# Two narrow weight sums moved behind the low halves of a group's plain slots

## The reference

```python
def hybrid_layer(x, ...):
    h = rms_norm(x, norm_mix)
    proj = h @ w_in                              # 2048 x 5656
    ...
    x = x + mix @ w_out                          # 2048 x 2048
    hf = rms_norm(x, norm_ffn)
    gate, up = jnp.split(hf @ w_gu, 2, axis=-1)  # 2048 x 11264
    return x + (jax.nn.silu(gate) * up) @ w_down # 5632 x 2048
```

## Time and profile before

| what | value |
|---|---|
| time, median of 3 executions | 1097.41 us (1097.21 to 1098.8) |
| the profiled execution | 1097.72 us, span 1096.0 us |
| TensorE busy | 1084.9 us, 5071 matmuls |
| VectorE busy | 888.4 us, 1092 instructions |
| ScalarE busy | 598.8 us, 736 instructions |
| TensorE's granted clock | 0.999 of full speed |
| `raw` loads of `w_gu` | 176, 512 KB each, median 4.2 us from issue to landing |
| `raw` loads of `w_down` | 88, 512 KB each, median 4.6 us |

### The profile page before, as it was taken

One profiled execution on the slowest core, in us unless ns is written; L12 is line 12 of the kernel. 1 busy time (PEld: TensorE's weight loads), 2 busy tenths in 40 slices (PEclk: granted clock), 3 DMA queues, 4 the chain that ended last, 5 costly groups with the idle time before them and its releaser, 6 DMA issues.

```text
span 1096.0 us, 13959 instructions
## 1 busy us (share of the span) xinstructions
PE 1084.9 (99%) x5071; PEld 902.9 (82%) x5071; DVE 888.4 (81%) x1092; ACT 598.8 (55%) x736; POOL 40.7 (4%) x68
## 2 busy tenths in 40 slices
PE   9999999999999999999999999999999999999997
PEld 7897889888888888888888888888888878888885
DVE  5556866688756557999999999999998999899896
ACT  5655545555545445555655555556556555646553
POOL 2600000000010000000000000000000000000000
PEclk9999999999999999999999999999999999999999
DMA  8665646565546675656566566556666856666663
GB/s 290 214 199 168 186 131 179 161 173 154 181 163 235 188 253 171 204 185 210 189 199 214 165 208 206 185 184 209 210 192 197 301 190 215 203 200 209 200 224 117
DMA packets 110948, 215.39 MB, mean 197 GB/s; under 512 B 6957, under 2 KB 11633, under 8 KB 110001
## 3 DMA queue, kind: packets, MB, share of 16 engines
q1 hardware_dynamic: 108976, 205.36, 59.1%
q0 software_dynamic: 1632, 8.96, 2.2%
q10 hardware_dynamic: 288, 0.39, 0.1%
HBM read 210.49 MB, written 4.19 MB: 196 GB/s over the span
## 4 chain that ended last, share of the span: by engine, by line
PE 92%; DVE 4%; DMA 2%; issue 1%; ACT 1%; SPq 0%; POOLq 0%; POOL 0%; DVEq 0%; ACTq 0%
PE acc L1454 11%; PE acc L1455 11%; PE acc L1456 11%; PE acc L1735 10%; PE acc L1734 10%; PE acc L1736 10%; PE acc L1805 4%; PE acc L1807 4%; PE acc L1806 4%; PE mx L1734 3%; PE mx L1735 2%; PE mx L1736 2%; PE mx L1446 2%; PE mx L1805 1%; PE mx L1807 1%; PE mx L1806 1%
## 5 line engine op out<-in xcount | busy, mean ns | idle before, releaser
L786 DVE TENSOR_TENSOR w_lo<-raw,w_hi 128x1024 fp32r<-128x1024 f32 (+2 forms) x144 | 166.4, 1169 | 120.2 <-ACT w_hi L473 119.5
L473 ACT ACTIVATE w_hi<-raw 128x1024 fp32r<-128x1024 f32 (+2 forms) x143 | 143.2, 1013 | 135.4 <-PE acc L1456 129.0
L1734 PE MATMUL acc<-w_hi,hT_hi 128*128 128x512 f32 x460 | 179.9, 391 | 0.0
L1735 PE MATMUL acc<-w_lo,hT_hi 128*128 128x512 f32 x460 | 179.1, 389 | 0.0
L1736 PE MATMUL acc<-w_hi,hT_lo 128*128 128x512 f32 x460 | 179.0, 389 | 0.0
L1221 DVE TENSOR_TENSOR w_lo<-raw,w_hi 128x1024 fp32r<-128x1024 f32 (+1 forms) x160 | 173.3, 1119 | 2.8
L673 ACT ACTIVATE w_hi<-raw 128x1024 fp32r<-128x1024 f32 (+1 forms) x160 | 151.5, 978 | 36.7 <-PE acc L1736 21.8
L1454 PE MATMUL acc<-w_hi,hT_hi 128*128 128x512 f32 (+2 forms) x416 | 157.7, 379 | 0.0
L1456 PE MATMUL acc<-w_hi,hT_lo 128*128 128x512 f32 (+2 forms) x416 | 155.5, 374 | 0.0
L1455 PE MATMUL acc<-w_lo,hT_hi 128*128 128x512 f32 (+2 forms) x416 | 155.5, 374 | 0.0
L679 ACT ACTIVATE w_hi<-ff_sum 128x1024 fp32r<-128x1024 f32 x60 | 63.8, 1063 | 78.3 <-PE acc L1736 65.2
(11 more groups left out here) (317 smaller groups left out, 1682.5 us busy)
## 6 DMA issues: line engine op xcount, KB each, us to landing
raw<-in_w_gu SPq DMA_DIRECT2D x176, 512.0 KB, 4.2
raw<-in_w_down SPq DMA_DIRECT2D x88, 512.0 KB, 4.6
raw<-in_w_in SPq DMA_DIRECT2D x79, 512.0 KB, 4.0
raw<-in_w_out SPq DMA_DIRECT2D x32, 512.0 KB, 4.3
raw<-in_w_in SPq DMA_DIRECT2D x8, 272.0 KB, 2.8
raw<-in_w_in SPq DMA_DIRECT2D x8, 264.0 KB, 2.8
x<-in_x POOLq DMA_DIRECT2D x2, 1024.0 KB, 9.5
x_kept<-x POOLq DMA_DIRECT2D x2, 1024.0 KB, 7.3
```

The costliest lines, as they stand in the source:

```text
L786: dve.tensor_tensor(w_lo[:, slot, 0:UC * width], raw[:, slot, 0:UC * width], w_hi[:, slot, 0:UC * width].bitcast(F32), ALU.subtract).then_ ...
L1734: pe.matmul(o, a[0], w[0], start=first, stop=False)
L1735: pe.matmul(o, a[0], w[1], start=False, stop=False)
```

## The change

VectorE's order within a group changes. `ff_weight_sums` and `weight_sums` keep the wide sum alone. The two narrow sums become functions of their own, `ff_last_sums` and `last_sums`, which are called behind the low halves of the group's two plain slots and ahead of the low half of the wide sum. In the FFN's first group the activation sums (`act_sums`, `act_low`) keep their place ahead of the plain slots' low halves, so they now follow the wide sum directly. As the narrow sums read the raw slots after the low halves do, SyncE waits for the last sum as well before it loads into a raw slot of a group. The two tables `FF_SUMS_OF` and `SUMS_OF` say which loads that are, and the count to wait for.

```diff
--- before.py
+++ after.py
@@ -69,6 +69,7 @@
     FF_SLOT_OF[_i] = _v
     if _kind == "seven":
         FF_SLOT_OF[_i + 1] = _v + 1
+FF_SUMS_OF = {_i + d: 2 * _k + 2 for _kind, _k, _i, _v in FF_ORDER if _kind == "seven" for d in range(2)}
 
 
 def lin(j, m, c=0):
@@ -137,6 +138,8 @@
     SLOT_OF[_q] = _v
     if _kind in ("pair", "seven"):
         SLOT_OF[_q + 1] = _v + 1
+SUMMED_AT = [_q for _kind, _half, _k, _q, _v in DOWN if _kind == "seven"]
+SUMS_OF = {_q + d: 2 * n + 2 for n, _q in enumerate(SUMMED_AT) for d in range(2)}
 LAST_SEVEN = [max(i for i, d in enumerate(DOWN) if d[0] == "seven" and d[1] == h) for h in range(2)]
 FIRST_RIGHT = [i for i, d in enumerate(DOWN) if d[1] == 1][0]
 SPLIT = [(0, 5), (5, 7), (7, SUMMED)]
@@ -321,6 +324,9 @@
                 load(w_gu, U_FF + k, k % R, (k % UPG) * UC * P, FF if k >= UPG else 0, GW)
 
             def load_ff(j, k, i, up):
+                summed = FF_SUMS_OF.get(i - R)
+                if summed is not None:
+                    sp.wait_ge(sem("ff_w_sums"), (j - 1) * 2 * FF_SUMMED + summed)
                 sp.wait_ge(lo_ready, j * FF_SLOTS + (FF_BASE + FF_SLOT_OF[i - R] + 1))
                 sp.dma_start(raw[:, i % R, :].rearrange("p (k n) -> p k n", k=UC),
                              weights(w_gu, k * UC * P, j * GW + (FF if up else 0), GW)).then_inc(loaded[i % R], 16)
@@ -334,6 +340,8 @@
                         load_ff(j, k, i, kind == "up")
 
             def load_down(n, k, q):
+                if q - R in SUMS_OF:
+                    sp.wait_ge(sem("w_sums"), SUMS_OF[q - R])
                 sp.wait_ge(lo_ready, SLOT_OF.get(q - R, V_DN + q - R - U_DN) + 1)
                 sp.dma_start(raw[:, q % R, :].rearrange("p (k n) -> p k n", k=UC),
                              weights(w_down, k * UC * P, n * GW, GW)).then_inc(loaded[q % R], 16)
@@ -1242,6 +1250,10 @@
                 upper = raw[:, a:a + 2, 0:GW] if b > a else raw[:, a::b - a, 0:GW]
                 dve.tensor_tensor(ff_sum[:, 0, :, :], raw[:, b, :].rearrange("p (k n) -> p k n", k=UC), upper,
                                   ALU.subtract).then_inc(sem("ff_w_sums"), 1)
+
+            def ff_last_sums(j, i, k):
+
+                a, b = i % R, (i + 1) % R
                 dve.wait_ge(sem("ff_w_sums"), lin(j, 2 * FF_SUMMED, 2 * (k - FF_SUMMED) + 1))
                 dve.tensor_tensor(ff_sum[:, 1, 0, :], raw[:, b, GW:2 * GW], ff_sum[:, 0, 0, :], ALU.subtract)\
                    .then_inc(sem("ff_t2"), 1)
@@ -1281,6 +1293,7 @@
                     ff_low(j, i, v)
                     if kind == "seven":
                         ff_low(j, i + 1, v + 1, GW)
+                        ff_last_sums(j, i, k)
                         ff_sum_low(j, 0, v + 2)
                         ff_sum_low(j, 1, v + 3)
                     if kind == "gate" and k == 4:
@@ -1338,6 +1351,10 @@
                 dve.wait_ge(loaded[a + 1], 16 * (q // R + 1))
                 dve.tensor_tensor(gate_s[:, :, :], raw[:, a + 1, :].rearrange("p (k n) -> p k n", k=UC),
                                   raw[:, a:a + 2, 0:GW], ALU.subtract).then_inc(sem("w_sums"), 1)
+
+            def last_sums(q, made):
+
+                a = q % R
                 dve.wait_ge(sem("actT_psum"), NG_FF)
                 dve.wait_ge(sem("w_sums"), made - 1)
                 step(dve.tensor_tensor(act_tok[:, 0, :], raw[:, a + 1, GW:2 * GW], gate_s[:, 0, :], ALU.subtract))
@@ -1397,6 +1414,7 @@
                         for b in range(NB):
                             down_add(0, b, v - 2)
                     down_low(v + 1, q + 1, GW)
+                    last_sums(q, 2 * sevens)
                     sum_low(v + 2, gate_s)
                     if i == FIRST_RIGHT:
                         for b in range(NB):
```

## The result

| kernel | median | runs | range |
|---|---|---|---|
| before | 1097.31 us | 6 | 1096.54 to 1098.8 us |
| changed | 1101.93 us | 6 | 1101.28 to 1102.83 us |

The ratio is 1.0041, 95% interval 1.003 to 1.0051. The change costs 4.6 us where the forecast's case said +1.3. The time lies inside the predicted range (1093.8 to 1103.5), but beyond the 2.2 us that were called "same", and outside the forecast case's own range (1096.5 to 1100.5). It is the outcome "slower", which had 0.32. The profiled execution took 1101.67 us, with a span of 1099.9 us and a granted clock of 0.998.

What follows compares the result with a forecast made beforehand. TensorE, busy 1084.9 of 1096.0 us, was taken to bound the kernel, so only its waits could change. Third groups -3.5, first groups +4.8 and down stage 0 made +1.3 us on 1097.4: 1098.7 us, range 1093.8 to 1103.5.

Steps and rivals of the forecast that it cites:

- the forecast's case: Whole kernel: +1.3 us, to 1098.7 us, with its own range 1096.5 to 1100.5; chance 0.60.
- slower: Whole kernel: outcome of a slowdown beyond the 2.2 us a measurement can tell from no change; chance 0.32.
- Loads set the pace: FFN loop and down stage: loads released later hold up the next group's sums; likely 1101 to 1104 us, chance 0.27.
- Third groups: Third group of each FFN pass: first slot ready 1.45 us earlier, ending ten waits of 0.35 us; -3.5 us.
- First groups: First group of nine FFN passes: narrow sums lose their cover, third slot is late, 0.53 us each; +4.8 us.
- Now VectorE idles until 692.00: FFN first group: VectorE waits behind the wide sum for ScalarE's copies, ending at 691.97, before the activation sums start.
- Order within a group: VectorE, from the wide sum's start: third slot ready after 5.43 us instead of 5.55, first after 2.36 instead of 3.81.
- Later release in the FFN loop: FFN loop: second group's loads wait for narrow sums; third group's third slot keeps a 0.2 us margin, costed at nothing.
- Down stage: Down stage: second group's wait moves from first slot to third; bounds -1.0 and +1.5 us, taken as 0.
- The wait just goes: First group's third slot is in time after all, if ready 0.36 us earlier; 1093 to 1094 us, chance 0.13.
- The ring: Down stage: issue, landing and sums total 9.6 us at median landing, against TensorE's 10.2; binds when landings exceed 5.2 us.
- The profile I had asked for: Signs of right: third-group waits gone, nine new first-group waits about 0.4 us, VectorE idle, down-stage wait at wide sum's low half.

Runs made afterwards that it cites:

- e11: Kernel before with the new order in the third group of each FFN pass only; 1094.62 us, ratio 0.9975.
- e4: Changed kernel with the FFN's hardware loop over the middle eight passes written out; 1098.66 us, ratio 1.001.
- e5: Kernel before with the FFN's hardware loop written out; 1098.05 us, ratio 1.0004.
- e6: e3 with ScalarE's copy for the down stage moved one up slot earlier; 1094.58 us, ratio 0.9966.
- e1: Changed kernel with the change kept in the FFN loop only, the down stage as before; 1102.46 us, ratio 1.004.
- e12: Kernel before, order unchanged, with only a group's first raw slot released 0.6 us later, together with its second; 1098.82 us, ratio 1.0015.
- e10: Kernel before, order unchanged, with both raw slots of a group reloaded only once the third slot's low half is made; 1145.19 us, ratio 1.0428.
- e2: Changed kernel with the change kept in the down stage only, the FFN loop as before; 1097.55 us, ratio 0.9999.
- e7: Kernel before with the change in third groups of the FFN loop and in the down stage; 1095.07 us, ratio 0.9978.
- e3: Changed kernel, but in each pass's first group both narrow sums and the raw slot releases stand as before; 1094.63 us, ratio 0.9972.
- e8: Changed kernel, but in first groups narrow sum 1 alone goes ahead of the activation sums, narrow sum 2 staying behind the low halves; 1094.97 us, ratio 0.9977.
- e9: e3 with the FFN's hardware loop written out; 1093.53 us, ratio 0.9966.

## Why the prediction was right in its mechanism and short in its size

- **The number.** 1101.93 is inside the stated range in part by luck. The forecast's case ended at 1100.5; the range went further for the rival "Loads set the pace" (1101 to 1104), whose mechanism is not what made the time.
- **Third groups.** Right. All ten waits are gone, -3.3 us against -3.5. e11 has this part alone and is 3.0 us faster than before.
- **First groups.** The mechanism, place and count are right: nine passes pay, the last does not, no second wait follows. The size is off: 0.75 to 0.81 us in eight of them against 0.53. The step that failed is "Now VectorE idles until 692.00". I took the start behind ScalarE's copy as 0.03 after its end. Measured are 0.25 in the loop and 0.10 with constants (e4). Together with a low half that reached TensorE after 0.13 instead of 0.06 in every other pass, this is about the 1.8 us between 4.8 and 6.6. e4 with e5 shows that the loop's form of the code makes it: -3.3 us for writing out the changed kernel, +0.3 (nothing) for the kernel before. The 0.03 was right for an instruction that carries its wait itself (L1227); this one has a wait and a register instruction in front.
- **Order within a group.** Right. From the earlier trace rows I worked out 4.29 us from the wide sum's start to the end of the narrow ones and 5.43 to the third slot. In the down stage it is 884.17 + 0.69 - 880.57 = 4.29, and 884.78 + 1.22 - 880.57 = 5.43:

```profile
880.57 1.23 DVE L1352 TENSOR_TENSOR gate_s<-raw 128x1024 f32<-128x1024 f32 x1 [0.68 <-DMA raw<-in_w_down]
881.71 1.82 DVE L1334 TENSOR_TENSOR w_lo<-raw,w_hi 128x1024 fp32r<-128x1024 f32 x2
883.45 0.68 DVE L1360 TENSOR_TENSOR act_tok<-raw,gate_s 128x512 f32<-128x512 f32 x1
884.17 0.69 DVE L1362 TENSOR_TENSOR act_tok<-raw,act_tok 128x512 f32<-128x512 f32 x1
884.78 1.22 DVE L1340 TENSOR_TENSOR w_lo<-gate_s,w_hi 128x1024 fp32r<-128x1024 f32 x1
```

- **Later release in the FFN loop.** I gave the third group a margin of 0.2 us and costed it at nothing. That held in eight passes. In pass 1 it did not (0.4), in pass 4 not quite (0.1), and one up slot of pass 2 was late (0.3): a small miss.
- **Down stage.** Costed at nothing. The load of the second group landed after 5.0 us this time, not 6.8, and the third slot was ready at 886.00, 1.05 us ahead of TensorE (887.05). So here the wait did not move to the third slot, as I had it. In e6, where the same load took 6.37 us, it did: its wide sum started at 873.76, and 5.43 + 0.06 later is 879.25; TensorE started that slot at 879.24, after a wait of 0.33. The mechanism was right, and the landing decides. It decides in the old order too. This one load took 6.80 us before, 6.54 in e1, 6.40 in e5, 5.60 in e12 and 5.25 in e11, and the wait at the first slot was 0.97, 0.71, 0.56, 0.19 and none. (In e10 the load is issued later as well.) With the new order it took 5.0 to 6.4 us, and no profile has that wait. So the 1.1 us that the profiles show against the kernel before are in part that one slow landing in its profiled execution; e11 shows them as well, with the old order in the down stage. The wait of the first pair, 0.1 to 0.8 us, differs in the same way, without an edit that explains it (0.11 before, 0.70 in e5). The medians show no gain of the new order there (e2 by itself, e7 against e11). How often the landing is slow outside the profiled executions stays open.
- **The rival "The wait just goes".** It needed the slot 0.36 us earlier; the slot came later than I had it. What this rival described is what e3 and e11 measured, 1094.6 us.
- **The rival "Loads set the pace".** Not the cause: e8 has the late loads without the loss, and the changed kernel's third groups wait in two of ten passes only, 0.5 us together. But it was not far. The ring with the new order is 0.03 + 0.60 + 5.0 + 0.12 + 4.29 = 10.0 us for a landing of 5.0, against 10.2. e10, with a down-stage ring 1.3 us longer (11.4), lost 47 us. The Trainium skill (DMA: Bandwidth & Descriptors, "Rules for kernel authors") advises to issue early and wait late. e10 agrees with it past that edge, and e8 and e12 show that short of it a later issue costs almost nothing.
- **The profile I had asked for.** All of the signs of "right" appeared but one: no wait moved to the down stage's third slot. The nine new waits were 0.6 to 0.7 us in the loop, not 0.4.

The better kernel changes the order only where TensorE waited: e11 with 1094.62 us. Its other forms, e3, e6 and e9, lie between 1093.5 and 1094.6 us, 2.9 to 4.1 below their "before", and their intervals overlap with that of e11.

## What to carry to other kernels

Before work is moved behind a slot, ask what it covered where it stood: here the same two instructions were in TensorE's way in one group and filled an idle time in another. What an idle engine needs to start behind another depends on what its sequencer does after the wait: 0.03, 0.10 and 0.25 us here, in the same loop. So cost a new idle time by a row with the same instructions between wait and start. For each release made later, work the whole ring out and set it against the busiest engine's period, as in the down stage here it cost next to nothing up to that edge and 1.2 to 1.3 us in each round past it.

## What the runs showed of the hardware

- Behind a wait for another engine VectorE started 0.25 us after the releasing instruction's end inside a hardware loop, and 0.10 us after it in code written out, for the same instruction; ScalarE 0.40 to 0.42 against 0.31. A register instruction of 0.09 us between wait and start, which the written-out code does not have, is most of VectorE's difference; without one, VectorE started after 0.03 or 0.10 us inside the loop too (L1235, L1270). Where VectorE was busy, the time showed none of this (e5: no change).
- Each wait of TensorE, however short, cost a restart of 0.08 to 0.17 us: the first matmul behind it takes 0.31 to 0.34 us to the next start instead of 0.227.
- VectorE's independent instructions of 128 x 1024 elements start some 0.08 us before the end of the one ahead, in the changed kernel too (880.57 + 1.23 = 881.80, next start 881.71).
- The landing of one and the same load of 512 KB took 5.0 to 6.8 us over the profiles, and TensorE's wait behind it, in the old order, went from none (5.25) to 0.97 us (6.80).
- Loads held back by 1.1 to 1.7 us cost 47 us of 1098 (e10); one load of each pair held back by 0.6 us cost about 1 us (e12).
